# Gated activations made during gate/up by GpSimd and ScalarE: one change to a tuned decoder layer on one core

## The reference

```
h    = rmsnorm(x, ffn_norm)
gate = h @ w_gate                 # 2048 x 5632
up   = h @ w_up                   # 2048 x 5632
x    = x + (silu(gate) * up) @ w_down
out  = rmsnorm(x, final_norm)
```

## Time and profile before

| | |
|---|---|
| median of 3 runs | 1979.11 us (1978.85 to 1979.38) |
| profiled execution: span, first to last instruction | 1977.3 us |
| what the median has beyond the span | 1.8 us |
| busy: TensorE, its weight loads | 1967.3 us (99%), 1691.6 us (86%) |
| busy: VectorE, ScalarE, GpSimd | 1654.7 (84%), 1126.6 (57%), 167.2 (8%) us |
| mean granted TensorE clock | 0.999 of full speed |

### The profile page before, as it was taken

The page is one execution under the profiler, slowest core; times in us unless marked ns, Lnnn a source line. Parts: engine busy times, 40 slices in busy tenths (PEclk is TensorE's granted clock), DMA queues, the critical chain, the costliest instruction groups (busy, mean ns, idle before and its releaser), DMA issues.

```text
span 1977.3 us, 29282 instructions
## 1 busy us (share of the span) xinstructions
PE 1967.3 (99%) x10300; PEld 1691.6 (86%) x10300; DVE 1654.7 (84%) x2386; ACT 1126.6 (57%) x2064; POOL 167.2 (8%) x261
## 2 busy tenths in 40 slices
PE   9999999999999999999999999999999999999998
PEld 7888888888888988888888888888888888888886
DVE  8877767777766999999999999999998688697886
ACT  6566666666346655555646555555556355566643
POOL 5002333223100000000000000000000000000000
PEclk9999999999999999999999999999999999999999
DMA  9322222224334344443434344444347836546433
GB/s 343 127 83 70 70 71 70 69 70 139 102 117 138 119 148 137 130 139 130 137 132 142 131 134 135 136 139 135 132 138 238 303 120 227 176 148 221 126 130 133
DMA packets 132889, 276.16 MB, mean 140 GB/s; under 512 B 13392, under 2 KB 13424, under 8 KB 131744
## 3 DMA queue, kind: packets, MB, share of 16 engines
q1 hardware_dynamic: 120896, 239.65, 37.9%
q0 software_dynamic: 6640, 23.82, 3.1%
q10 hardware_dynamic: 5232, 11.04, 1.6%
HBM read 242.99 MB, written 31.46 MB: 139 GB/s over the span
## 4 chain that ended last, share of the span: by engine, by line
PE 96%; DVE 2%; issue 1%; DMA 1%; ACT 0%; SPq 0%; POOLq 0%; POOL 0%; DVEq 0%; ACTq 0%
PE bank L841 25%; PE bank L844 13%; PE bank L702 7%; PE bank L768 7%; PE bank L770 7%; PE bank L769 7%; PE bank L704 7%; PE bank L703 7%; PE bank L900 3%; PE bank L898 3%; PE bank L899 3%; PE bank L925 2%; PE bank L942 1%; PE bank L910 1%; PE bank L909 1%
## 5 line engine op out<-in xcount | busy, mean ns | idle before, releaser
L841 PE MATMUL bank<-s_two,t_hi 128*128 128x512 f32 x2352 | 557.3, 390 | 0.0
L1485 ACT ACTIVATE t_hi<-t_raw 128x1792 fp32r<-128x1792 f32 x176 | 302.5, 1720 | 358.1 <-DVE t_raw L2155 269.7
L841 PEld LDWEIGHTS bank<-s_two,t_hi 128*128 128x128 f32 x2352 | 433.5, 188 | 84.7
L2161 DVE TENSOR_TENSOR t_lo<-t_raw,t_hi 128x1792 fp32r<-128x1792 f32 x176 | 355.7, 2021 | 20.7 <-ACT t_hi L1485 20.6
L844 PEld LDWEIGHTS bank<-s_two,t_lo 128*128 128x128 f32 x2352 | 298.9, 191 | 10.4 <-DVE t_lo L2161 0.6
L844 PE MATMUL bank<-s_two,t_lo 128*128 128x256 f32 x2352 | 302.1, 283 | 0.4 <-DVE t_lo L2161 0.4
L1136 ACT ACTIVATE w_hi<-raw 128x512 fp32r<-128x512 f32 x268 | 168.8, 631 | 189.5 <-PE bank L770 141.4
L1778 DVE TENSOR_TENSOR w_lo<-raw,w_hi 128x512 fp32r<-128x512 f32 x268 | 184.6, 690 | 56.6 <-ACT w_hi L1136 56.0
L2152 DVE TENSOR_TENSOR t_raw<-t_raw 128x1024 f32<-128x1024 f32 x176 | 215.0, 1221 | 17.2 <-DMA t_raw<-in_w_gu 15.5
L702 PE MATMUL bank<-h_hi,w_hi 128*128 128x512 f32 x416 | 166.0, 399 | 1.1 <-DVE h_lo L1782 0.6
L704 PE MATMUL bank<-h_lo,w_hi 128*128 128x512 f32 x416 | 162.6, 391 | 0.0
(11 more groups left out here) (260 smaller groups left out, 3487.8 us busy)
## 6 DMA issues: line engine op xcount, KB each, us to landing
t_raw<-in_w_gu SPq DMA_DIRECT2D x348, 256.0 KB, 2.8
raw<-in_w_down SPq DMA_DIRECT2D x112, 256.0 KB, 3.6
raw<-in_w_in SPq DMA_DIRECT2D x104, 256.0 KB, 2.7
gu_mid<-part POOLq DMA_DIRECT2D x43, 512.0 KB, 2.9
gu_next<-gu_mid SPq DMA_DIRECT2D x36, 512.0 KB, 6.9
raw<-in_w_out SPq DMA_DIRECT2D x64, 256.0 KB, 3.0
fast_y<-in_w_down SPq DMA_DIRECT2D x24, 512.0 KB, 5.0
fast_z<-in_w_down SPq DMA_DIRECT2D x16, 512.0 KB, 4.7
```

The costliest lines, as they stand in the source:

```text
L841: mm = nc.tensor.matmul(b[:, :], t_hi[r][:, ti, q, :], both, start=d == 0 and q == 0, stop=d == DOUBLES - 1 and q == 1 and i < 4, skip_gro ...
L1485: nc.scalar.activation(t_hi[r][:, :, :, :].rearrange("p a q c -> p (a q c)"), t_raw[r][:, 1:8, :, :].rearrange("p a q c -> p (a q c)"), AC ...
L2161: nc.vector.tensor_tensor(t_lo[r][:, :, :, :].rearrange("p a q c -> p (a q c)"), t_raw[r][:, 1:8, :, :].rearrange("p a q c -> p (a q c)"), ...
```

## The change

The gate of a tile is scaled, passed through Silu and multiplied by up right behind `post`, while gate/up goes on. GpSimd does the two multiplications (from `part`, or `part_low` for tile 1), ScalarE the Silu in place at the first double of the group after next (at double 13 for tiles 0 and 1). The product goes to one of two tiles `act_out`, and only this, 256 KB, is stored in `gu_mid`; `take_products` waits for GpSimd's product of the tile before (`act_done`) instead of for a store. In down the loads bring 256 KB and the three steps are gone from VectorE's and ScalarE's queues; `down_high` and `a_sums` wait for the load itself. The first load of a tile in down comes behind the first four w_down loads and `t_low` of double 174. r2 is spread 16 doubles sooner: the means at double 8, the widening at 9, TensorE's turn at 9, the copy at 12. The Silu table is loaded ahead of the loops of gate/up.

```diff
-SPREAD_T = 25
+SPREAD_T = 9
+    act_out = [sb(f"act_out{b}", [P, SEQ], at=place_ez + 7168 + 2048 * b) for b in range(2)]
-    gu_s = [sb(f"gu_s{k}", [P, 2, SEQ], at=places_u[k]) for k in range(CHUNK)]
+    gu_s = [sb(f"gu_s{k}", [P, SEQ], at=places_u[k]) for k in range(CHUNK)]
...
# SyncE
-        sp.wait_ge(rbc_ready, 2)
-        load_gu(0, 0)
         sp.wait_ge(t_lo_done, ALL_T - 2)
         for s in range(4):
             load_down(0, s)
-        for k in (1, 2):
+        for k in (0, 1, 2):
             sp.wait_ge(t_lo_done, ALL_T - 1)
             load_gu(0, k)
...
# ScalarE
             if stored_too:
-                act.wait_ge(gu_stored, 16 * g)
+                act.wait_ge(act_done, g)
...
+        def silu(g):
+
+            gate = products_of(g)[:, 0:2, :]
+            act.wait_ge(gs_done, g + 1)
+            nc.scalar.activation(gate, gate, ACT.Silu).then_inc(silu_done, 1)
...
+                if first and j == SPREAD_T + 4:
+                    silu(0)
+                    silu(1)
+                if j % 4 == 0 and not (first and j < 16):
+                    silu(LOOP_G * i + j // 4 - 2)
...
# VectorE
-                if first and j == 14:
+                if first and j == 8:
                     row_means(2)
-                if first and j == 17:
+                if first and j == 9:
...
-        def gate_scaled(i, k):
-
-            dve.wait_ge(gu_loaded[k], 16 * (i + 1))
-            gate = gu_tile(i, k)[:, 0, :]
-            nc.vector.tensor_tensor(gate, gate, r2_bc[:, :], ALU.mult).then_inc(gs_done, 1)
-
-        def gate_times_up(i, k):
-
-            dve.wait_ge(silu_done, 8 * i + k + 1)
-            gu = gu_tile(i, k)
-            nc.vector.tensor_tensor(gu[:, 0, :], gu[:, 0, :], gu[:, 1, :], ALU.mult).then_inc(act_done, 1)
...
# GpSimd
-            nc.gpsimd.dma_start(gu_mid[g, :, :], z[:, 0:4, :].rearrange("p a c -> p (a c)")).then_inc(gu_stored, 16)
...
+        def gate_scaled(g):
+
+            gate = products_of(g)[:, 0:2, :]
             pool.wait_ge(post_done, POSTS * (g + 1))
+            if g == 0:
+                pool.wait_ge(rbc_done, 2)
+            nc.gpsimd.tensor_tensor(gate, gate, r2_bc[:, :].rearrange("p (a c) -> p a c", c=HALF), ALU.mult).then_inc(gs_done, 1)
+
+        def gate_times_up(g):
+
+            z, dst = products_of(g), act_out[g % 2]
+            pool.wait_ge(silu_done, g + 1)
+            if g > 1:
+                pool.wait_ge(gu_stored[g % 2], 16 * (g // 2))
+            nc.gpsimd.tensor_tensor(dst[:, :].rearrange("p (a c) -> p a c", c=HALF), z[:, 0:2, :], z[:, 2:4, :], ALU.mult).then_inc(act_done, 1)
+            pool.wait_ge(act_done, g + 1)
+            nc.gpsimd.dma_start(gu_mid[g, :, :], dst[:, :]).then_inc(gu_stored[g % 2], 16)
+
+        gate_scaled(0)
+        gate_scaled(1)
+        gate_times_up(0)
+        gate_times_up(1)
+        for g in range(2, TILES):
+            gate_scaled(g)
+            gate_times_up(g)
```

More of the change, by code:

```diff
@@ L308, in build @@
     prod_ready, bank_taken, folded, post_done = sem("prod_ready"), sem("bank_taken"), sem("folded"), sem("post_done")
-    gu_stored = sem("gu_stored")
+    gu_stored = [sem(f"gu_stored{b}") for b in range(2)]
     gu_loaded = [sem(f"gu_loaded{k}") for k in range(CHUNK)]
@@ L414, in gu_tile, with products_of @@
     def gu_tile(i, k):
-        return gu_s[k][:, :, :] if i == 0 else gu_next[:, k, :, :]
+        return gu_s[k][:, :] if i == 0 else gu_next[:, k, 0, :]
+    def products_of(g):
+        return part_low if isinstance(g, int) and g == 1 else part
     def unit_of(c, s):
@@ L646, in _ @@
                 load_quarter("z", raw_z, 1, s - 26, 2, 2)
-        sp.wait_ge(gu_stored, 16 * TILES)
+        for b in range(2):
+            sp.wait_ge(gu_stored[b], 8 * TILES)
         for s in range(7):
@@ L1514, in take_products @@
                 if p == 0:
-                    slots_free(i, gj, isinstance(g, int) and g == 2)
+                    slots_free(i, gj, False)
                     if not (isinstance(g, int) and g == 2):
@@ L1616, in _ @@
             six_groups(i)
[L1617 to L1620 removed]
         def down_high(i, k):
[L1624 removed]
+            act.wait_ge(gu_loaded[k], 16 * (i + 1))
             if i == 0:
@@ L1691, in down_first @@
                 if s == 28:
-                    act.wait_ge(gu_stored, 16 * TILES)
+                    for b in range(2):
+                        act.wait_ge(gu_stored[b], 8 * TILES)
                 if s in (28, 29):
@@ L1735, in _ @@
         split(U_DOWN // 4, 2)
[L1736 to L1739, removed]
+        take_products(7, 1)
         down_first()
@@ L2171, in post @@
                 dve.wait_ge(folded, g - 1)
-            z = part_low if isinstance(g, int) and g == 1 else part
+            z = products_of(g)
             nc.vector.tensor_tensor(z[:, 1, :], z[:, 1, :], z[:, 5, :], ALU.add).then_inc(post_done, 1)
@@ L2610, in _ @@
         invert(2, slice(0, 2 * NT))
-        def store_gu(g):
+        invert(3, slice(0, NT))
+        def gate_scaled(g):
+            gate = products_of(g)[:, 0:2, :]
             pool.wait_ge(post_done, POSTS * (g + 1))
-            z = part_low if g == 1 else part
-            nc.gpsimd.dma_start(gu_mid[g, :, :], z[:, 0:4, :].rearrange("p a c -> p (a c)")).then_inc(gu_stored, 16)
-        for g in range(TILES):
-            store_gu(g)
-            if g == 1:
-                invert(3, slice(0, NT))
+            if g == 0:
[16 more added lines that the diff above has]
+            gate_times_up(g)
         for t in range(NT):
@@ L2671 @@
     args["x_mid"] = nc.dram_tensor("x_mid", (SEQ, D), F32, kind="Internal").ap()
-    args["gu_mid"] = nc.dram_tensor("gu_mid", (TILES, P, 2 * SEQ), F32, kind="Internal").ap()
+    args["gu_mid"] = nc.dram_tensor("gu_mid", (TILES, P, SEQ), F32, kind="Internal").ap()
     args["out"] = nc.dram_tensor("out_x", (1, SEQ, D), F32, kind="ExternalOutput").ap()
```

50 lines of the change are left out of this document (12 added, 38 removed).

## The result

The changed kernel takes 2050.46 us (median of 4 runs, 2049.48 to 2051.47), the kernel before on the same chip 1979.24 (4 runs, 1978.85 to 1979.69). The ratio is 1.0361 (95% interval 1.0346 to 1.0375): 71 us slower, at a granted clock of 0.999. The profiled execution's span is 2049.6 us, 72.3 more than before.

What follows compares the result with a forecast made beforehand. TensorE's instruction stream bounds the kernel; with GpSimd's holds VectorE becomes gate/up's bound. 46 (period) + 7 (late loads) + 2 (start) = 55 us on the 1977.3 span, plus 1.8 to the median: 2034 us, range 2006 to 2058.

Steps and rivals of the forecast that it cites:

- rival B: Gate/up: GpSimd keeps the port from issue to end, 2.58 us a group, total 2056 us; chance 0.08.
- 46 for the period: Gate/up: VectorE becomes the bound, period 20.62 us, +1.15 a group over 40 groups, 46 us.
- 7 for late loads: Gate/up: t_raw loads that come late now and then show once VectorE bounds; 3 to 10 us, taken as 7.
- 2 for the start: Start of gate/up: four GpSimd instructions come together beside the third group; 0 to 4 us, taken as 2.
- The price, 1.02: Gate/up: each GpSimd tensor_tensor holds the shared SBUF port against VectorE for 1.02 us, 2.04 a group.
- I take 0.2: Gate/up, t_raw ring: wait for loads before a group's fourth t_sums, 0 to 0.25 us more a group, taken as 0.2.
- within the 1.09 above: Gate/up: VectorE's 19.2 us of t_hi waits counted inside its room of 1.09 us a group, filled by GpSimd's instructions.
- Nothing for the down stage: Down: VectorE is relieved of 61 us, but TensorE covers it without a wait, so no gain.
- The signs named ahead: Profile after: TensorE waits for t_lo some 50 us in all; VectorE near 100% busy, no t_hi waits, two instructions longer by 1.0.
- C: Gate/up: GpSimd's instructions cost VectorE below 0.55 us each, TensorE stays the bound, 1979 us; chance 0.09.
- D: Gate/up: ScalarE's take_products is held for GpSimd's product; at 1 us a group adds 40, 2074 us; chance 0.05.
- E: Whole kernel: faster by over 4 us, 1969 to 1975, through unnamed TensorE waits fed by VectorE's 61 us; chance 0.03.

Runs made afterwards that it cites:

- 2: The kernel before with two GpSimd tensor_tensor of 128x512 a group added on a scratch tile, nothing of the computation changed: 2034.24 us, ratio 1.0278.
- 3: The changed kernel with GpSimd's two multiplications replaced by memsets of the same tiles, which read nothing: 1979.68 us, ratio 1.0003.
- 8: The changed kernel with only the first half of each w_gu load made in the loops: 2052.78 us, ratio 1.0370.
- 9: The changed kernel with ScalarE's copies of a group's first three products put ahead of the second double's t_high: 2043.90 us, ratio 1.0323.
- 1: The kernel before with only the sooner spreading of r2: 1979.21 us, ratio 1.0000.
- 12: The kernel before with two GpSimd tensor_scalar of 128x512 (one input tile, in place) a group added: 1999.46 us, ratio 1.0104.
- 10: The changed kernel with half of each gate/up weight load and the first three products' copies ahead of the second double's t_high: 2032.71 us, ratio 1.0268.
- 4: The changed kernel with both multiplications on VectorE inside gate/up, GpSimd only storing: 2003.79 us, ratio 1.0126.
- 11: The kernel before with three GpSimd tensor_tensor of 128x512 a group added, one tile as both inputs: 2063.35 us, ratio 1.0425.

## Why the prediction was right, and where it was off

**Right by its mechanism.** It said slower, because GpSimd and VectorE take turns at SBUF when both read there and VectorE reads two tiles, which makes VectorE the bound of gate/up. 2 shows the cost without the change, 3 the change without the cost. The measured 2050.5 lies in the range of 2006 to 2058, 16 us above the 2034, and just outside the forecast's own range (2016 to 2046): it is inside the stated one because that was widened to take in rival B.

**The terms.** The prediction had 46 for the period, 7 for late loads, 2 for the start and 1.8 from span to median. Measured: 64.8, 5.0, 4.3, -1.8 at the end of gate/up, and 0.9 from the span to the median. The difference, 18.8 - 2.0 + 2.3 - 1.8 - 0.9, is the 16.4 us. So it lies in the period: 1.62 a group where I had 1.15.

- *The price, 1.02: mis-sized by 0.08, 0.17 a group.* It was 1.10. From the VectorE instructions of rows 7 I had the right end, 0.13 before GpSimd's (GpSimd ends at 1110.21 + 2.19 = 1112.40, and L2158, which needs 0.42, gets going at 1112.68 - 0.42 = 1112.26). I had also taken 0.13 off the front. By starts, what was left off is 1.29 - 0.13 - 1.10 = 0.06. My estimate of why: successive VectorE instructions overlap by 0.08, and a hold takes that from the follower.
- *"I take 0.2" for the load wait: this is the step that failed, 0.3 of the 0.47 us a group.* 0.24 was there, as a row. But it was not a term to be added by itself, as 8 and 9 show: without it the wait for `t_hi` takes its place, and the two together, with the lost overlaps, are 0.49. I had written that the waits for `t_hi` are "within the 1.09 above", as room that GpSimd's instructions fill. They are room only where the delay doesn't reach ScalarE or shorten the time of a load. Here `t_high` waits for the delayed `t_sums`, with fourteen copies in its queue behind it. The prediction followed what waits for VectorE on TensorE, and not on ScalarE.
- *Nothing for the down stage, for Silu, for the spreading, for loads and stores:* right (1, 3). 61 us of relief are worth nothing where TensorE had no wait.
- *The start, 0 to 4 taken as 2:* 4.3. Four GpSimd instructions come together, and `take_products` of the third group stops at its fourth product for `act_done`, from 713.96 to 716.48:

```profile
712.29 1.87 POOL L2598 TENSOR_TENSOR act_out<-part 128x512 f32<-128x512 f32 x1 [1.16 <-ACT part L1607]
...
715.12 1.28 POOL L2598 TENSOR_TENSOR act_out<-part_low 128x512 f32<-128x512 f32 x1
```
```profile
717.19 2.39 PE L845 MATMUL bank<-s_two,t_hi 128*128 128x512 f32 x8 [2.04 <-ACT part L1529]
```

**The signs named ahead.** TensorE's wait for `t_lo` came 40 times at the place named, 37.4 us in all where 50 were forecast. Two VectorE instructions a group are longer by 1.09, where 1.0 was forecast. VectorE is busy for 621.7 of 640 us, not near 100%, and it still waits for `t_hi` (6.9 us, 26 times), where none was forecast: the same step that failed.

**The rivals.** *B* (issue to end, 2056) is nearer in time and still falls: a hold is 1.10 of 1.29 us in the changed kernel, 0.84 of 1.11, and 0.42 of 0.69. The holds are read from VectorE's rows; GpSimd's lengths are the profile's, which are rough, so how the rest splits between their two ends is not shown. The Trainium skill ("SBUF — State Buffer", section SBUF: two separate sides) says that the later one is blocked for the whole instruction. By these rows that has the kind right and is 0.2 to 0.3 us too long in each. *C* (not slower) falls, and its point of decision was wrong: 0.55 us each was worked out from the room of 1.09; 12 shows a loss at 0.43. With 0.6 of room it is near 0.3 for holds in this place, which no run here tried. *D* (ScalarE held for GpSimd's product) happened once, in the third group. Later the product is there in time (GpSimd's ends at 1116.90, the copies begin at 1118.83), and ScalarE is late for VectorE's sake. *E* (faster) falls: TensorE had nothing to give back.

**Left open.** The late groups (four of 22.5 to 22.8 us in the kernel after, about eight groups apart) were not traced to a cause. With half of each load (8) the late ones are 21.4 to 21.9 us, which points at the loads. In 9 and 10 TensorE still waits for `t_lo` in 39 and 38 groups, since VectorE's own 20.59 us are over its 19.47. No version tried beats the kernel before; 3, which reaches it, leaves the work out.

## What to carry to other kernels

Before work is moved to an idle engine, ask what it takes from the busy one: here 1.10 us for each instruction that VectorE does itself in 0.60 or 0.73, while writes alone took nothing. Even on VectorE the work cost 24 us in gate/up (4), more than its removal from down gave, which was nothing. The room of an engine is the period less its own work only when its waits would vanish if it were late; follow them first, and each queue that stands behind what it delays. How much of it is usable depends on where the new work stands: 0.6 us for GpSimd's holds here, all of 1.09 for VectorE's own multiplications in 4. And where two loops close at the same period, taking away one wait shows nothing: open both before you call either harmless.

## What was not expected of the hardware

- GpSimd's tensor_tensor of 128x512 takes 1.11 us with one tile as both inputs and 1.37 with two tiles, in the same place beside VectorE, and holds VectorE for 0.84 and 1.10 us. Subtraction and multiplication are alike.
- The hold doesn't depend on what VectorE runs: instructions of 0.42, 2.02 and 1.21 us (11) all grow by 0.84 or 0.85.
- A GpSimd instruction that finds VectorE in the middle of one waits for its end and then goes ahead of VectorE's next, which had been in the queue: two back to back (2) delayed two VectorE instructions in succession by one turn each, not one of them by both. This is what the traces show in the groups behind the start, but not always: at the start of gate/up in 8 one GpSimd instruction let seven of VectorE's go first and took 8.97 us.
